# Expert choice and slot computation in fewer dependent rounds, four position products for nine, the first gather ahead of the block list

## The chip, the cores and the metric

One core of one Trainium2 chip runs the whole kernel. The metric is the device time of one execution in microseconds. Its engines are TensorE (PE, matrix products; PEld is its loading of weights), VectorE (DVE), ScalarE (ACT), GpSimd (POOL) and SyncE (SP, which here only starts transfers); they run their own instruction streams and meet at semaphores.

## What is computed

One layer of a decoder on 320 tokens (256 of a prompt, 8 x 8 of samples): conditioning, a pooling and an RWKV-7 mixer, and a mixture of experts, all in float32. The change touches the routing of the mixture of experts, which reads in the reference:

```python
scores = sigmoid(h @ w_router)                        # (320, 16)
sel = scores + b_router
gscore = sum(top_k(sel.reshape(T, 4, 4), 2)[0], -1)   # the two best of each group of four
gbest = argmax(gscore, -1)
_, idx = top_k(where(in_group, sel, -inf), 2)         # the two best experts of the best group
wts = take_along_axis(scores, idx, 1); wts = wts / sum(wts)
...
dest = pstart[e_sorted] + (arange(A) - start[e_sorted])    # a slot for each token and expert
block_e = searchsorted(pend, arange(n_blocks) * block)     # the expert of each block
xb = h[toks]
y = (silu(xb @ w_gate[e]) * (xb @ w_up[e])) @ w_down[e]    # 2048 -> 1024 -> 2048
```

Ties go to the lower index, in the group as among the experts. The kernel uses blocks of 64 slots. With these inputs every expert has one block, so that 16 blocks are computed, and w_gate, w_up and w_down of each of the 16 experts (8.4 MB a matrix) are read once.

## The kernel before

Everything around the change lies in `phase_mix`. It has two `nc.Block()`s, at L1451 and L1799. At the end of a block all engines drain and meet in a barrier; at the start of the second each loads a loop count from `bei` (L1800, L1801), which VectorE has written before.

**First block.** TensorE multiplies by w_out (L1520), transposes back, and the second norm follows. `mg` holds the normed tokens with features in partitions. L1572 computes the router's logits, L1577 transposes them, L1585 transposes `mg` into token rows, which ScalarE copies to `h2` (L1638, twelve copies, semaphore `hb_ev`). VectorE (L1696 to L1784) does the routing. Its helper `step(ins)` issues one instruction and waits until it is complete; `o.did(ins)` issues without waiting, and `o.settle()` waits for all that were issued. A **round** is what lies between two such waits. Tokens lie in partitions, in three tiles of 128, 128 and 64.

- *Choice* (L1703 to L1736): sums with the bias, group scores from maxima and minima of pairs (L1706 to L1716), their maximum (L1718), the first group that equals it, by a serial loop over four groups (L1722, L1723), the rank of each expert in its group by a loop over four experts (L1727, L1731), and `chosen`, ones and zeros of 3 x 16 per partition (L1735, and L1736, which clears the rows beyond the last token). Then `ch_ok`.
- *Position products* on TensorE (L1593, L1596): for each tile, how many earlier tokens chose the expert (`tri`, strictly triangular, and `ones`), and the totals. Meanwhile VectorE normalises the weights (L1738 to L1745).
- *Slots* (L1750 to L1780): blocks per expert, their running sum, the list of blocks `bei` for all engines, `dest`, and the two slots `d01` of every token; then the two weights `w01` of every token (L1782 to L1784).

**Second block.** VectorE's `picks(b)` (L1969 to L1977) turns `d01` into a selection matrix `pick` for the 64 slots of block b, in two rounds. TensorE's `gather(b)` (L1836) multiplies it with `h2`; ScalarE copies the result to `xs` (L1924, L1925), TensorE transposes it (L1845), VectorE copies it to `xt` (L1983), and the expert's products with gate and up follow (L1868), then those with down (L1901). Blocks are taken in pairs, and block b + 1 is gathered inside block b. After each pair `send_back` (L1855), VectorE (L1992) and GpSimd (L2075) add the results to the residual.

**Weights.** SyncE loads the 12 units of each block in order (L1421) into a ring of six; each load waits for `used` of its slot, which TensorE raises with the last product that reads the unit. The first six units are loaded during the first block of instructions, the seventh waits for the first expert products of the second.

## Time and profile before

| | us |
|---|---|
| three timed runs | 1896.6, 1899.9, 1900.6 |
| median | 1899.9 |
| profiled execution, its own time | 1895.1 |
| span of the profiled execution | 1893.6 |
| choice, products and slots, first VectorE work to last | 895.2 to 912.8 |
| expert loop, first expert product to the end | 927.6 to 1893.6 |

TensorE is busy for 93% of the span, VectorE for 28%, ScalarE for 18%, GpSimd for 17%. Times of rows count from the start of the span. In a row of the order of time stand the start, the duration of the group, the engine, the line, the operation with what it writes and reads, the shape (partitions x elements) and how many instructions the group has; in brackets, how long the engine had been idle and who ended that. "Clock" is the clock granted to TensorE: 1.00 is its upper level, 2.4 GHz, and 0.50 its lower, 1.2 GHz.

### The profile page before, as it was taken

To read this page: it belongs to the slowest core of one execution; us is meant where nothing else is said; L and a number is where in the kernel's file an instruction comes from. 1 tells how busy PE (TensorE), PEld (TensorE's weight loads), DVE (VectorE), ACT (ScalarE), POOL (GpSimd) and SP (SyncE) were. 2 spreads that over 40 slices of the span, in tenths; PEclk is the share of its full clock that TensorE was granted. 3 is DMA by queue.
4 is the path that set the end of the run, shared out by engine and by line. 5 is a ranking of instruction groups with operands and counts; after the bars stand their busy time and mean duration, and the time that the engine had idled before them with its cause. 6 is when DMAs were issued, how large, how long until landed. Compare 5 with 4: busy or idle time off the path is not lost.

```text
span 1893.6 us, 28830 instructions
## 1 busy us (share of the span) xinstructions
PE 1768.3 (93%) x11589; PEld 919.5 (49%) x11589; DVE 529.9 (28%) x1239; ACT 334.1 (18%) x715; POOL 323.0 (17%) x474
## 2 busy tenths in 40 slices
PE   4799999999999997998699999999999999999996
PEld 1357655556555664775243343533535335353352
DVE  2225146555655451113211201112011120111203
ACT  2001223332333231005011000110001100011012
POOL 0030012211222022000000402204022040220403
PEclk9899999999999998998899999999999999999998
DMA  9984277656576546741299999999999999999992
GB/s 315 409 313 121 66 223 232 215 166 211 184 247 187 172 141 173 228 155 45 95 428 428 427 427 428 428 429 429 421 427 430 427 428 421 430 427 428 430 425 106
DMA packets 172632, 573.94 MB, mean 303 GB/s; under 512 B 10643, under 2 KB 102125, under 8 KB 146883
## 3 DMA queue, kind: packets, MB, share of 16 engines
q1 hardware_dynamic: 168750, 563.76, 76.7%
q0 software_dynamic: 3200, 6.20, 1.1%
q10 hardware_dynamic: 631, 3.27, 0.6%
q8 instruction: 36, 0.59, 0.1%
q14 instruction: 15, 0.12, 0.0%
HBM read 567.78 MB, written 5.65 MB: 303 GB/s over the span
## 4 chain that ended last, share of the span: by engine, by line
PE 39%; DMA 6%; issue 4%; POOL 1%; ACT 1%; DVE 0%; POOLq 0%; SPq 0%; DVEq 0%
PE PS L1868 18%; PE PS L1901 10%; DMA ring<-in_w_up 6%; PE PS L1836 5%; PE PS L1855 4%; PE PS L1845 1%; POOL x L2075 1%; PE PS L1891 1%; ACT xs L1925 0%; ACT xs L1924 0%; POOLq L1787 0%; POOL pw L2061 0%; SPq L1421 0%; DVE x L2035 0%; DVE xt L1983 0%
## 5 line engine op out<-in xcount | busy, mean ns | idle before, releaser
L1868 PE MATMUL PS<-ring,xt 128*64 128x512 f32 x2048 | 492.3, 603 | 26.3 <-DMA ring<-in_w_up 24.7
L1868 PEld LDWEIGHTS PS<-ring,xt 128*64 128x64 f32 x2048 | 196.8, 138 | 288.1 <-issue 243.5
L2075 POOL TENSOR_TENSOR x<-x,tmp 128x512 f32<-128x512 f32 (+1 forms) x96 | 125.2, 1307 | 668.5 <-DVE tmp L1992 668.5
L1901 PE MATMUL PS<-ring,att 128*64 128x512 f32 x1024 | 227.5, 593 | 0.0
L753 PE MATMUL PS<-ring 128*64 128x320 f32 x1344 | 219.4, 440 | 2.7 <-DMA ring<-in_w_in 2.7
L1901 PEld LDWEIGHTS PS<-ring,att 128*64 128x64 f32 x1024 | 116.8, 137 | 95.6 <-issue 58.3
L1992 DVE TENSOR_TENSOR tmp<-PS,catT 128x512 f32<-128x512 f32 (+1 forms) x96 | 66.1, 689 | 299.7 <-PE PS L1855 296.2
L2003 DVE TENSOR_TENSOR sgt<-sgt,PS 64x1024 f32<-64x1024 f32 x16 | 19.4, 1212 | 424.6 <-ACT sgt L1931 424.6
L1520 PE MATMUL PS<-catT,ring 128*128 128x320 f32 x416 | 114.4, 437 | 7.1 <-DMA ring<-in_w_out 7.1
L1836 PE MATMUL PS<-h,pick 128*64 128x512 f32 x408 | 107.5, 600 | 10.4 <-DVE pick L1973 10.4
L753 PEld LDWEIGHTS PS<-ring 128*64 128x64 f32 x1344 | 82.3, 138 | 62.9 <-issue 25.4
L1931 ACT ACTIVATE sgt<-PS 64x1024 f32<-64x1024 f32 x16 | 16.3, 1017 | 538.8 <-PE PS L1868 538.8
L1855 PE MATMUL PS<-ysb,pwt 128*128 128x512 f32 (+1 forms) x192 | 105.5, 636 | 5.3 <-DVE tmp L1992 2.5
L2061 POOL TENSOR_SCALAR pw<-slotw,d,w 128x64 f32<-128x64 f32 x96 | 55.4, 592 | 277.0 <-issue 175.3
L1520 PEld LDWEIGHTS PS<-catT,ring 128*128 128x128 f32 x416 | 79.4, 192 | 40.8 <-issue 9.1
L1836 PEld LDWEIGHTS PS<-h,pick 128*64 128x64 f32 x408 | 40.6, 138 | 73.6 <-issue 63.1
L1942 ACT COPY ysb<-PS 64x1024 f32<-64x1024 f32 x32 | 32.2, 1007 | 212.8 <-PE PS L1901 212.6
L1855 PEld LDWEIGHTS PS<-ysb,pwt 128*128 128x128 f32 (+1 forms) x192 | 28.2, 173 | 77.0 <-issue 66.1
L419 PE MATMUL PS<-ring,silT 128*32 128x512 f32 x512 | 61.6, 598 | 0.0
L722 POOL TENSOR_TENSOR uvx<-uv,bmask 128x512 f32<-128x512 f32 x16 | 16.3, 1035 | 254.1 <-DVE uv L1318 254.1
L1110 ACT COPY zbd<-PS 64x320 f32<-64x320 f32 x80 | 33.5, 419 | 143.5 <-PE PS L902 143.0
L1269 DVE COPY_PREDICATED invt<-lvl_t,PS 64x320 f32<-64x320 int32 x80 | 41.4, 518 | 18.2 <-PE PS L902 14.9
(451 smaller groups left out, 1831.7 us busy)
## 6 DMA issues: line engine op xcount, KB each, us to landing
ring<-in_w_gate SPq DMA_DIRECT2D x64, 2048.0 KB, 12.5
ring<-in_w_up SPq DMA_DIRECT2D x64, 2048.0 KB, 16.2
ring<-in_w_down SPq DMA_DIRECT2D x64, 2048.0 KB, 15.7
ring<-in_w_ada SPq DMA_DIRECT2D x43, 2048.0 KB, 11.1
ring<-in_w_in SPq DMA_DIRECT2D x28, 1024.0 KB, 8.3
ring<-in_w_out SPq DMA_DIRECT2D x16, 1024.0 KB, 8.4
catT<-in_w_ada SPq DMA_DIRECT2D x5, 2048.0 KB, 11.5
ring<-in_w_in SPq DMA_DIRECT2D x1, 3072.0 KB, 20.4
```

What stands on the lines that cost most here:

```text
L419: m = nc.tensor.matmul(psum[32 * g:32 * g + 32, :], silT[:, kt, :], abuf[:, u, k, :], start=(kt < 4), stop=(kt >= KT - 4))
L753: m = nc.tensor.matmul(PS[r, j, 0:T], wbuf[:, j, k, r], hT[:, k, :], start=(k == 0), stop=(k == KT - 1), skip_group_check=True)
L1110: m = nc.scalar.copy(zbd[r, :, h, :], cut(W[3][r, 0:T]))
L1269: return nc.vector.copy_predicated(dst, nc_, src)
L1520: m = nc.tensor.matmul(PS[:, j, 0:T], wo[:, j, k, :], catT[:, k, :], start=(k == 0), stop=(k == KT - 1))
L1836: m = nc.tensor.matmul(PS[C * (c % 2):C * (c % 2) + C, 4 + c // 2, :], pick[:, i, :], h2[:, i, 512 * c:512 * c + 512], start=(i == 0), sto ...
L1855: nc.tensor.matmul(PS[0:n_, 2 + r % 2, :], pwt[:, t0:t0 + n_], ysb[:, c, :], start=True, stop=True).then_inc(t_sc, 1)
L1868: m = nc.tensor.matmul(PS[C * g:C * g + C, c, :], xt[:, 4 * q + k, :], unit(2 * q + g, FE)[:, k, 512 * c:512 * c + 512], start=(q == 0 and ...
L1901: m = nc.tensor.matmul(PS[C * (c % 2):C * (c % 2) + C, 4 + c // 2, :], att[:, 2 * q + k, :], unit(u, D)[:, k, 512 * c:512 * c + 512], star ...
L1992: nc.vector.tensor_tensor(tmp[0:n_, r % 2, :], PS[0:n_, 2 + r % 2, :], gtm[0:n_, i // 2, 512 * c:512 * c + 512], ALU.mult).then_inc(sc_ev, 1)
L2061: m = nc.gpsimd.tensor_scalar(pw[:, k, i, :], slotw[:, :], d01[:, k, i:i + 1], w01[:, k, i:i + 1], ALU.is_equal, ALU.mult)
L2075: nc.gpsimd.tensor_tensor(xx, xx, tmp[0:n_, r % 2, :], ALU.add).then_inc(x_ok, 1)
```

## The change

- *Choice*: all comparisons of the four experts of a group with each other are made at once, 12 x 4 x 4 = 192 elements per partition, once "greater" (`over`) and once "equal" (`same`, kept where the rival has the lower index, `lower`); their sum over the rivals is the rank. The first best group comes from a product with 4, 3, 2, 1 (`first`) and a maximum. The rows beyond the last token are cleared in `rank`, beside another operation. VectorE waits for GpSimd's set-up earlier. Rounds up to `ch_ok`: 11 for 26.
- *Products*: four with up to 48 columns, in place of nine with 16; the totals stand per tile and are summed by VectorE.
- *Slots*: blocks per expert by one comparison with five thresholds (`steps`) and a sum; near and far slots side by side; `picks(0)` at once behind `d01`, and the block list and the weights `w01` behind `picks(0)`. From the totals to `pick`, 12 rounds in place of 25.
- *Gather*: `gather(0)` stands at the end of TensorE's first block, with a wait for ScalarE's twelfth copy to `h2`; so the barrier and the loads of the loop count, which stood ahead of `picks(0)` and `gather(0)`, stand behind both.
- `gather` and `picks` are moved up so that both blocks can call them, unchanged but for the engine as an argument. `be` now lies in a part of `gated_tile`.

```diff
@@ -1423,6 +1423,29 @@
+    def gather(pe, b):
+        pe.wait_ge(pick_ok, b + 1)
...
+    def picks(ve, b):
+        earlier(ve, t_pk, b)
...
@@ -1435,11 +1458,16 @@
-    cmp_ = mt("cmp", [P, 12, EPG])
+    over, same = mt("over", [P, 12, EPG, EPG]), mt("same", [P, 12, EPG, EPG])
+    lower, first, steps = mt("lower", [P, EPG, EPG]), mt("first", [P, NG]), mt("steps", [P, T // SLOT])
+    count = mt("count", [P, NE])
+    flat = over[:, :, :, :].rearrange("p a e j -> p (a e j)")
+    full = flat[:, 0:NE * (T // SLOT)].rearrange("p (e k) -> p e k", e=NE)
+    near, far = (flat[:, n:n + 3 * NE].rearrange("p (i e) -> p i e", i=3) for n in (96, 144))
...
-    be = mt("be", [1, 32, NE])
+    be = gated_tile[0:1, 1:3, :].rearrange("p j t -> p (j t)")[:, 0:32 * NE].rearrange("p (b e) -> p b e", b=32)
@@ -1502,6 +1530,13 @@
+            own(nc.gpsimd.memset(lower[:, :, :], 0.0))
+            for e in range(1, EPG):
+                own(nc.gpsimd.memset(lower[:, e, 0:e], 1.0))
+            for g in range(NG):
+                own(nc.gpsimd.memset(first[:, g:g + 1], float(NG - g)))
+            for k in range(T // SLOT):
+                own(nc.gpsimd.memset(steps[:, k:k + 1], float(k * SLOT if k else -1)))
             pool.sem_inc(p_own, 1)
@@ -1588,13 +1623,16 @@
-            for i in range(3):
-                for i2 in range(i + 1):
-                    nc.tensor.matmul(PS[:, 7, i * NE:(i + 1) * NE], tri[:, :] if i2 == i else ones[:, :],
-                                     chosen[:, i2, :], start=(i2 == 0), stop=(i2 == i))
-            for i in range(3):
-                m = nc.tensor.matmul(PS[:, 7, 48:64], ones[:, :], chosen[:, i, :], start=(i == 0), stop=(i == 2))
-            m.then_inc(t_pos, 1)
+            picked = chosen[:, :, :].rearrange("p i e -> p (i e)")
+            nc.tensor.matmul(PS[:, 7, 0:48], tri[:, :], picked, start=True, stop=False, skip_group_check=True)
+            nc.tensor.matmul(PS[:, 7, 16:48], ones[:, :], picked[:, 0:32], start=False, stop=False, skip_group_check=True)
+            nc.tensor.matmul(PS[:, 7, 32:48], ones[:, :], picked[:, 0:16], start=False, stop=True, skip_group_check=True)
+            nc.tensor.matmul(PS[:, 7, 48:96], ones[:, :], picked, start=True, stop=True, skip_group_check=True
+                             ).then_inc(t_pos, 1)
+
+            pe.wait_ge(hb_ev, 12)
+            gather(pe, 0)
+
@@ -1702,41 +1740,41 @@
+            rival = s4.unsqueeze(2).broadcast_to([P, 12, EPG, EPG])
+            mine = s4.unsqueeze(3).broadcast_to([P, 12, EPG, EPG])
             for n, (a, b, op) in enumerate(((0, 1, ALU.max), (0, 1, ALU.min), (2, 3, ALU.max), (2, 3, ALU.min))):
                 o.did(tt(r4[:, n, :], s4[:, :, a], s4[:, :, b], op))
-
-            o.did(nc.vector.memset(rank[:, :, :], 0.0))
-            o.did(nc.vector.memset(small[:, 1, :], 1.0))
+            o.did(tt(same[:, :, :, :], rival, mine, ALU.is_equal))
+            o.did(tt(over[:, :, :, :], rival, mine, ALU.is_gt))
             o.settle()
+            ve.wait_ge(p_own, 2)
             o.did(tt(r4[:, 4, :], r4[:, 0, :], r4[:, 2, :], ALU.max))
             o.did(tt(r4[:, 5, :], r4[:, 0, :], r4[:, 2, :], ALU.min))
             o.did(tt(r4[:, 6, :], r4[:, 1, :], r4[:, 3, :], ALU.max))
+            o.did(tt(same[:, :, :, :], same[:, :, :, :],
+                     lower[:, :, :].unsqueeze(1).broadcast_to([P, 12, EPG, EPG]), ALU.mult))
             o.settle()
-            step(tt(r4[:, 5, :], r4[:, 5, :], r4[:, 6, :], ALU.max))
-            step(tt(r4[:, 4, :], r4[:, 4, :], r4[:, 5, :], ALU.add))
+            o.did(tt(r4[:, 5, :], r4[:, 5, :], r4[:, 6, :], ALU.max))
+            o.did(tt(over[:, :, :, :], over[:, :, :, :], same[:, :, :, :], ALU.add))
+            o.settle()
+            o.did(tt(r4[:, 4, :], r4[:, 4, :], r4[:, 5, :], ALU.add))
+            o.did(nc.vector.tensor_reduce(rank[:, :, :], over[:, :, :, :], AX.X, ALU.add))
+            o.settle()
             gsc = r4[:, 4, :].rearrange("p (i g) -> p i g", g=NG)
-            step(nc.vector.tensor_reduce(small[:, 0, :], gsc, AX.X, ALU.max))
+            o.did(nc.vector.tensor_reduce(small[:, 0, :], gsc, AX.X, ALU.max))
+            o.did(nc.vector.memset(rank[C:P, 8:12, :], float(EPG)))
+            o.settle()
             eq = r4[:, 5, :].rearrange("p (i g) -> p i g", g=NG)
             step(tt(eq, gsc, small[:, 0, :].unsqueeze(2).broadcast_to([P, 3, NG]), ALU.is_equal))
-            for g in range(NG):
-                step(tt(eq[:, :, g], eq[:, :, g], small[:, 1, :], ALU.mult))
-                step(tt(small[:, 1, :], small[:, 1, :], eq[:, :, g], ALU.subtract))
-            for j in range(EPG):
-                for lo, hi, op in ((0, j, ALU.is_gt), (j + 1, EPG, ALU.is_ge)):
-                    if lo < hi:
-                        o.did(tt(cmp_[:, :, lo:hi], s4[:, :, j:j + 1].broadcast_to([P, 12, hi - lo]), s4[:, :, lo:hi], op))
-                o.settle()
-                for lo, hi in ((0, j), (j + 1, EPG)):
-                    if lo < hi:
-                        o.did(tt(rank[:, :, lo:hi], rank[:, :, lo:hi], cmp_[:, :, lo:hi], ALU.add))
-                o.settle()
-            step(ts(rank[:, :, :], rank[:, :, :], 2.0, None, ALU.is_lt))
+            step(tt(eq, eq, first[:, :].unsqueeze(1).broadcast_to([P, 3, NG]), ALU.mult))
+            step(nc.vector.tensor_reduce(small[:, 1, :], eq, AX.X, ALU.max))
+            step(tt(eq, eq, small[:, 1, :].unsqueeze(2).broadcast_to([P, 3, NG]), ALU.is_equal))
             c4 = chosen[:, :, :].rearrange("p i (g e) -> p (i g) e", e=EPG)
-            step(tt(c4, rank[:, :, :], r4[:, 5, :].unsqueeze(2).broadcast_to([P, 12, EPG]), ALU.mult))
-            step(nc.vector.memset(chosen[C:P, 2, :], 0.0))
+            step(nc.vector.scalar_tensor_tensor(out=c4, in0=rank[:, :, :], scalar=2.0,
+                                                in1=r4[:, 5, :].unsqueeze(2).broadcast_to([P, 12, EPG]),
+                                                op0=ALU.is_lt, op1=ALU.mult))
             ve.sem_inc(ch_ok, 1)
...
@@ -1745,43 +1783,48 @@
             ve.wait_ge(t_pos, 1)
-            ve.wait_ge(p_own, 2)
-            for k in range(T // SLOT):
-                step(nc.vector.scalar_tensor_tensor(out=nb[:, 0, :], in0=PS[:, 7, 48:64], scalar=float(k * SLOT),
-                                                    in1=nb[:, 0, :], op0=ALU.is_gt, op1=ALU.add))
-            step(ts(nb[:, 0, :], nb[:, 0, :], 1.0, None, ALU.max))
+            step(nc.vector.tensor_reduce(count[:, :], PS[:, 7, 48:96].rearrange("p (i e) -> p e i", i=3), AX.X, ALU.add))
+            step(tt(full[:, :, :], count[:, :].unsqueeze(2).broadcast_to([P, NE, T // SLOT]),
+                    steps[:, :].unsqueeze(1).broadcast_to([P, NE, T // SLOT]), ALU.is_gt))
+            step(nc.vector.tensor_reduce(nb[:, 0, :], full[:, :, :], AX.X, ALU.add))
             step(nc.vector.tensor_tensor_scan(nb[:, 1, :], nb[:, 3, :], nb[:, 0, :], 0.0, ALU.mult, ALU.add))
-            o.did(tt(nb[:, 2, :], nb[:, 1, :], nb[:, 0, :], ALU.subtract))
+            step(tt(nb[:, 2, :], nb[:, 1, :], nb[:, 0, :], ALU.subtract))
+            step(ts(nb[:, 2, :], nb[:, 2, :], float(SLOT), None, ALU.mult))
+            step(tt(dest[:, :, :], PS[:, 7, 0:48].rearrange("p (i e) -> p i e", e=NE),
+                    nb[:, 2, :].unsqueeze(1).broadcast_to([P, 3, NE]), ALU.add))
+            big = 8192.0
+            o.did(nc.vector.scalar_tensor_tensor(out=near[:, :, :], in0=dest[:, :, :], scalar=-big, in1=chosen[:, :, :],
+                                                 op0=ALU.add, op1=ALU.mult))
+            o.did(nc.vector.scalar_tensor_tensor(out=far[:, :, :], in0=dest[:, :, :], scalar=1.0, in1=chosen[:, :, :],
+                                                 op0=ALU.add, op1=ALU.mult))
+            o.settle()
+            o.did(nc.vector.tensor_reduce(d01[:, 0, :], near[:, :, :], AX.X, ALU.min))
+            o.did(nc.vector.tensor_reduce(d01[:, 1, :], far[:, :, :], AX.X, ALU.max))
+            o.settle()
+            o.did(ts(d01[:, 0, :], d01[:, 0, :], big, None, ALU.add))
+            o.did(ts(d01[:, 1, :], d01[:, 1, :], -1.0, None, ALU.add))
+            o.settle()
+            picks(ve, 0)
 
             o.did(tt(be[:, :, :], nb[0:1, 1, :].unsqueeze(1).broadcast_to([1, 32, NE]),
                      bnum[:, :].unsqueeze(2).broadcast_to([1, 32, NE]), ALU.is_le))
             o.did(tt(odd[:, :], bnum[:, 0:32:2], nb[0:1, 1, NE - 1:NE].broadcast_to([1, 16]), ALU.is_lt))
+            for v, k in ((near, 0), (far, 1)):
+                o.did(tt(v[:, :, :], dest[:, :, :], d01[:, k, :].unsqueeze(2).broadcast_to([P, 3, NE]), ALU.is_equal))
             o.settle()
-            o.did(ts(nb[:, 2, :], nb[:, 2, :], float(SLOT), None, ALU.mult))
             o.did(nc.vector.tensor_reduce(bef[:, :], be[:, :, :], AX.X, ALU.add))
             o.did(nc.vector.tensor_reduce(npair[:, 1:2], odd[:, :], AX.X, ALU.add))
+            for v in (near, far):
+                o.did(tt(v[:, :, :], v[:, :, :], wts[:, :, :], ALU.mult))
             o.settle()
             o.did(ts(npair[:, 0:1], npair[:, 1:2], 2.0, None, ALU.mult))
             o.did(ts(bef[:, :], bef[:, :], float(NE - 1), None, ALU.min))
-            o.did(tt(dest[:, :, :], PS[:, 7, 0:48].rearrange("p (i e) -> p i e", e=NE),
-                     nb[:, 2, :].unsqueeze(1).broadcast_to([P, 3, NE]), ALU.add))
+            for v, k in ((near, 0), (far, 1)):
+                o.did(nc.vector.tensor_reduce(w01[:, k, :], v[:, :, :], AX.X, ALU.add))
             o.settle()
             o.did(nc.vector.tensor_copy(bei[:, 0:32], bef[:, :]))
             o.did(nc.vector.tensor_copy(bei[:, 32:34], npair[:, :]))
-
-            big = 8192.0
-            step(ts(sel[:, :, :], dest[:, :, :], -1.0, big, ALU.mult, ALU.add))
-            step(tt(sel[:, :, :], sel[:, :, :], chosen[:, :, :], ALU.mult))
-            step(nc.vector.tensor_reduce(d01[:, 0, :], sel[:, :, :], AX.X, ALU.max))
-            o.did(ts(d01[:, 0, :], d01[:, 0, :], -1.0, big, ALU.mult, ALU.add))
-            step(ts(sel[:, :, :], dest[:, :, :], 1.0, None, ALU.add))
-            step(tt(sel[:, :, :], sel[:, :, :], chosen[:, :, :], ALU.mult))
-            step(nc.vector.tensor_reduce(d01[:, 1, :], sel[:, :, :], AX.X, ALU.max))
-            step(ts(d01[:, 1, :], d01[:, 1, :], -1.0, None, ALU.add))
-            for k in range(2):
-                step(tt(sel[:, :, :], dest[:, :, :], d01[:, k, :].unsqueeze(2).broadcast_to([P, 3, NE]), ALU.is_equal))
-                step(tt(sel[:, :, :], sel[:, :, :], wts[:, :, :], ALU.mult))
-                step(nc.vector.tensor_reduce(w01[:, k, :], sel[:, :, :], AX.X, ALU.add))
+            o.settle()
     mixing.close()
@@ -1827,16 +1870,6 @@
-            def gather(b):
...
@@ -1875,7 +1908,7 @@
-                gather(b + 1)
+                gather(pe, b + 1)
@@ -1905,7 +1938,6 @@
-            gather(0)
             gather_turn(0)
@@ -1962,21 +1994,6 @@
-            def picks(b):
...
@@ -1994,7 +2011,7 @@
-                picks(b + 1)
+                picks(ve, b + 1)
@@ -2009,7 +2026,6 @@
-            picks(0)
             turned(0)
```

## Rows read from the trace of the kernel before

**Rows 1.** Stretches: us, PE, PEld, DVE, ACT, POOL, clock, DMA share, GB/s

```profile
937.00:942.00 5.00, 5.00 (x26) 1.72 (x24) 0.00 (x0) 0.00 (x0) 0.00 (x0) 1.00 0.98 413
...
1001.00:1800.00 799.00, 779.96 (x3390) 348.99 (x3388) 128.94 (x238) 83.67 (x110) 167.80 (x196) 0.99 1.01 427
```

**Rows 2.** Who waited for whom, 920 to 1894: us in total, times, longest

```profile
PE PS L1868 <- DMA ring<-in_w_up: 24.7, 14, 2.7
```

**Rows 3.** Order of time, start of the expert loop: start, us, what, [idle before]

```profile
927.56 28.04 PE L1868 MATMUL PS<-ring,xt 128*64 128x512 f32 x128 [1.46 <-DVE xt L1983]
...
934.67 0.33 SPq L1421 DMA_DIRECT2D ring<-in_w_gate  x1
```

**Rows 4.** Order of time, choice of experts and the first position product

```profile
893.87 5.40 PE L1585 MATMUL PS<-ident,mg 128*128 128x128 f32 x48
...
895.07 5.84 ACT L1638 COPY h<-PS 128x512 f32<-128x512 f32 x12
895.20 0.21 DVE L1703 TENSOR_TENSOR sel<-scores,browt 128x48 f32<-128x48 f32 x1 [0.72 <-ACT scores L1633]
895.44 0.45 DVE L1706 TENSOR_TENSOR r<-sel 128x12 f32<-128x12 f32 x4
...
897.19 0.17 DVE L1722 TENSOR_TENSOR r<-r,small 128x3 f32<-128x3 f32 x1
897.39 0.16 DVE L1723 TENSOR_TENSOR small<-small,r 128x3 f32<-128x3 f32 x1
...
901.43 0.07 DVE L1736 MEMSET chosen<- 64x16 f32 x1
901.65 0.21 DVE L1738 TENSOR_TENSOR wts<-scores,chosen 128x48 f32<-128x48 f32 x1
...
901.71 0.37 PE L1593 MATMUL PS<-chosen,tri 128*128 128x16 f32 x2 [2.44 <-DVEq L1737]
```

**Rows 5.** Order of time, slots on VectorE

```profile
905.97 1.01 DVE L1750 SCALAR_TENSOR_TENSOR nb<-PS,nb 128x16 f32<-128x16 f32 x5 [3.17 <-PE PS L1596]
...
907.54 0.67 DVE L1756 TENSOR_TENSOR be<-nb,bnum 1x512 f32<-1x512 f32 x1
...
912.36 0.21 DVE L1783 TENSOR_TENSOR sel<-sel,wts 128x48 f32<-128x48 f32 x1
912.60 0.20 DVE L1784 TENSOR_REDUCE w<-sel 128x3 f32<-128x48 f32 x1
```

**Rows 6.** Order of time, selection matrices, gathers and the copy on ScalarE

```profile
914.31 0.70 DVE L1969 TENSOR_SCALAR pick<-slotf,d 128x64 f32<-128x64 f32 x3 [1.51 <-issue]
914.32 3.46 POOL L2061 TENSOR_SCALAR pw<-slotw,d,w 128x64 f32<-128x64 f32 x6 [175.34 <-issue]
...
915.90 7.81 PE L1836 MATMUL PS<-h,pick 128*64 128x512 f32 x24 [10.41 <-DVE pick L1973]
...
923.75 0.58 ACT L1924 COPY xs<-PS 128x512 f32<-128x512 f32 x1 [22.83 <-PE PS L1836]
...
927.42 0.57 DVE L1969 TENSOR_SCALAR pick<-slotf,d 128x64 f32<-128x64 f32 x3
...
955.39 6.23 PE L1836 MATMUL PS<-h,pick 128*64 128x512 f32 x24
```

**Rows 7.** Busy time by microsecond; the number before the DMA share is the clock

```profile
888.00:889.00 1.00, 1.00 (x5) 0.47 (x3) 0.00 (x0) 0.75 (x3) 0.00 (x0) 0.50 0.00 0
...
901.00:902.00 1.00, 0.29 (x3) 0.32 (x3) 0.72 (x7) 0.00 (x0) 0.00 (x0) 0.98 0.00 0
...
918.00:919.00 1.00, 1.00 (x4) 0.29 (x2) 0.00 (x0) 0.00 (x0) 0.80 (x2) 0.50 0.00 0
919.00:920.00 1.00, 1.00 (x6) 0.34 (x4) 0.00 (x0) 0.00 (x0) 0.05 (x1) 0.99 0.00 0
```

**Rows 8.** The block boundary (L1451): the drain of TensorE, duration in ns and start

```profile
L1451 PEldq DRAIN  x1: 3648/3648/3648, 901.9 to 901.9; - x1
```

**Rows 9.** The load of the loop count (L1801) on ScalarE

```profile
L1801 ACTq TENSOR_LOAD <-bei x1: 488/488/488, 913.3 to 913.3; - x1
```

More of the change, by code:

```diff
@@ L1736, in _ @@
-            step(nc.vector.memset(chosen[C:P, 2, :], 0.0))
+            step(nc.vector.scalar_tensor_tensor(out=c4, in0=rank[:, :, :], scalar=2.0,
+                                                in1=r4[:, 5, :].unsqueeze(2).broadcast_to([P, 12, EPG]),
+                                                op0=ALU.is_lt, op1=ALU.mult))
             ve.sem_inc(ch_ok, 1)
             o.did(tt(wts[:, :, :], scores[:, :, :], chosen[:, :, :], ALU.mult))
-            o.did(nc.vector.memset(nb[:, 0, :], 0.0))
@@ L1829, in _ @@
             n = pairs(pe)
-            def gather(b):
-                pe.wait_ge(pick_ok, b + 1)
-                for c in range(4):
-                    for i in range(3):
-                        m = nc.tensor.matmul(PS[C * (c % 2):C * (c % 2) + C, 4 + c // 2, :], pick[:, i, :],
-                                             h2[:, i, 512 * c:512 * c + 512], start=(i == 0), stop=(i == 2),
-                                             skip_group_check=True)
-                m.then_inc(t_pk, 1)
             def gather_turn(b):
```

29 lines of the change are left out of this document (17 added, 12 removed).

## The prediction

> **What bounds the kernel now.** I read three views, in this order. First the stretches of the expert loop [rows 1]: the DMA engines are busy for the whole of it (share 1.01) at 427 GB/s, and TensorE is busy for 780 of 799 us beside them. Both run close to full, so I then asked who waits for whom [rows 2]: TensorE waits for a weight transfer 14 times, 24.7 us in all. The loop is paced by its weights, and TensorE follows just behind. Nothing in the loop is changed, so the question is when it starts. Third, the order of time at its start [rows 3]: six of a block's twelve weight units lie in the ring beforehand; the seventh is asked for at 934.67, when TensorE has used up the first. From then on the DMA never rests (share 0.98 from 937 to 942, 1.01 later) [rows 1]. Hence the rule on which my sum rests: every microsecond by which the transfer of 934.67 starts earlier comes off the end of the kernel, and a microsecond saved on an engine later in the loop is worth nothing.
>
> What precedes 934.67 is one serial chain from 895.20, where VectorE gets the scores. In it the DMA moves nothing, so no transfer hides any of it. It has four links: choice of experts [rows 4], position products and slots [rows 5], the block boundary with the selection matrices and the gather [rows 6], and the copies, transposes and the first 16 expert products (32 instructions).
>
> **Prices on VectorE.** Two neighbouring rows give the price of a dependent round: 0.20 us with 3 elements per partition (897.19 to 897.39) [rows 4], 0.24 with 48 (912.36 to 912.60) [rows 5]. The operation with 512 elements took 0.67 against 0.21 for 48 [rows 5], so an element costs (0.67 − 0.21) / 464 = 1.0 ns. A round of 192 elements is then 0.24 + 0.144 = 0.39 us; of 80 elements, 0.27. Within a round an operation that waits for nobody takes 0.10 (12 elements, four in 0.45 [rows 4]), about 0.14 (48) or 0.28 (192): its duration less the part that overlaps, some 0.07 us.
>
> **Choice of experts.** Before: 895.20 to the first position product at 901.71, 6.51 us [rows 4]. After, from 895.20: sum with bias 0.24; four pair operations 0.41 plus two comparisons of 192 elements 0.28 + 0.39; three small ones 0.25 plus a product 0.39; two rounds of 0.08 + 0.39; the group maximum with the small memset beside it 0.22; four rounds of 0.20; the final choice 0.24. Sum: 4.16. From there to TensorE I take the old way, which is 0.20 (the memset ends at 901.50, the product starts at 901.71) [rows 4]. So 4.36, and the product starts at 899.56; **2.15 us saved**. The 192-element operations read with broadcasts over two inner dimensions, which no row shows. Lower bound 0 extra; upper bound, twice the price per element for the five of them, 5 x 0.19 = 1.0 us. I take 0, since the 512-element row is a broadcast too. TensorE is free then: its transposes end at 893.87 + 5.40 = 899.27 [rows 4]. The added wait on GpSimd's set-up is free: GpSimd has sat idle for 175 us by 914.32 [rows 6], and 13 small memsets before that use none of the path.
>
> **Position products.** Before: 901.71 to VectorE's first slot operation at 905.97, 4.26 us [rows 4, 5]: 18 matmul instructions (two for each of nine float32 products), and the clock falls to its lower level at 902 [rows 7]. After: four products, 8 instructions. While it has just been working at the upper level, TensorE passes a 128-column transpose every 5.40 / 48 = 0.11 us [rows 4]; 8 x 0.11 plus 0.2 for the last gives 1.1. VectorE meanwhile normalises the weights, five rounds of 0.24, 0.24, 0.20, 0.20 and 0.24, together 1.12, and the two end side by side. I take 1.15, **3.1 saved**. At the lower level an instruction takes (4.26 − 0.5) / 18 = 0.21, with 0.5 for the last one's end; 8 x 0.21 + 0.5 is 2.2, and the saving 2.05. I take the first, since the clock stood at the upper level until 902 after a rest of 2.4 us [rows 4, 7], and here the rest is 0.3.
>
> **Slots.** Before: 905.97 to the end of the last reduction at 912.80; the boundary, until 914.31; two rounds of selection matrices, until the gather starts at 915.90: 9.93 us [rows 5, 6]. After: count 0.24, thresholds 0.27, their sum 0.27, scan 0.23, subtract 0.20, times 64 0.20, destinations 0.22, near and far 0.38, two reductions 0.38, two corrections 0.28 = 2.67. Then the matrices: 1.59 before, when GpSimd worked beside VectorE; with GpSimd idle the three first operations took 0.57 in place of 0.70 [rows 6], so I take 1.37, with 1.59 as the other end. Together 4.04; **5.9 saved**. The block list and the weights of the slots, taken off this path, cost about 2.9 us of VectorE behind the matrices. They lie under the gather of 7.8 us; without that cover they would cost their 2.9.
>
> The gather would thus start 2.15 + 3.1 + 5.9 = 11.15 us earlier, at 904.75. h2 is complete by 895.07 + 5.84 = 900.91 [rows 4], so its new wait is free.
>
> **What comes back.** The block boundary is not gone, it moves behind the gather. Before, ScalarE copied the gather's result 0.04 us after it ended (915.90 + 7.81 to 923.75) [rows 6]. Now TensorE reaches the barrier last, and what is queued behind it on ScalarE is the load of the loop count and then that copy. VectorE was the last then: 1.5 us from its end at 912.80 to its work at 914.31 [rows 5, 6]. ScalarE's load stands at 913.3 and takes 0.49 [rows 9], so its work can start some 0.3 us before that of VectorE, whose own end also took longer to be told than TensorE's: the drain of TensorE lasts just until its products are done (901.9 + 3.65 = 905.55) [rows 8]. Bounds 0.9 and 1.5 us. I take 1.15 more than before. GpSimd now builds its slot weights while VectorE copies the transposed tokens (1.29 us); by the ratio 0.70 / 0.57 that is up to 0.3, and I take 0.1, as that copy reads PSUM.
>
> **Sum:** 11.15 − 1.15 − 0.1 = **9.9 us**, with the gather as long as before. The gather ran its first three microseconds at the lower clock, until 919 [rows 7], and this adds 7.81 − 6.23 = 1.6 us against a later one [rows 6]. It now follows a rest of 4.1 us in place of 10, and can be anything from 6.2 to about 8.3. I keep 7.8.
>
> **The clock behind the gather.** From the gather's end to the first expert product, TensorE had only eight transposes in 3.8 us (923.71 to 927.56) [rows 3, 6], and what came next ran at the upper level's pace from the start (128 instructions in 28.04). The boundary stretches that to 5.0 us. In the rows the clock stood at the lower level during a microsecond full of transposes of h (888 to 889), yet it was still at the upper one at 901 to 902, behind 5.4 us of transposes of mg and 2.4 us of rest [rows 4, 7]. The Trainium skill (TensorE: Matmul & The Clock Gate, Part 4: PE-mode transpose) says that transposes don't count as work for the clock; by it the whole 5.0 us are rest and a fall is likely. The trace agrees for the rise and speaks against it for the fall.
>
> **Rivals.** (1) *The clock falls in those 5.0 us.* Then about 1.7 to 3.4 us of the first expert products, which release the seventh transfer, run at half speed: 0.8 to 1.7 lost, saving 8.6. For it: the longer rest. Against: the rows of 893 to 902. (2) *Cheap rounds are dearer than their small neighbours.* The five wide operations cost 1.0 more, the products run at the lower level (1.05 more), boundary and copies are at their dear ends (0.55), the clock falls too (1.3): saving 6.0. (3) *The gain is swallowed by a clock that stays low.* With less than full work between 899 and 917, the lower level could hold through gather and first products. The gather then takes 12.5 in place of 7.8, the first 16 products 14.0 in place of 7.0 (927.56 to 934.67, less 0.1) [rows 3], the small steps 0.3 more: 12.0, and the kernel is 2 us slower. If the level holds through the next 16 as well, ring slots come free 14.0 us apart while two units take 9.8 us (a unit is a quarter of an 8.4 MB matrix, and the rate 427 GB/s), the DMA starves for 4.2 more, and the kernel is 6 us slower. It decides from some 11 us of dense products at the lower level; the rows show 3 [rows 7]. (4) *The change doesn't shorten the start*, because the loop waits for something else. Against it stands the transfer of 934.67, issued when the 16th product ends (32 of the 128 instructions of 28.04 us are 7.0) and not before [rows 3]; 0 saved.
>
> **How the numbers follow.** Profiled execution: span 1893.6, time 1895.1, so 1.5 lie around it; after, span 1883.7 and 1885.2. The three timed runs have their median at 1899.9, 4.8 above the profiled one, and I forecast on that basis: 1899.9 − 9.9 = **1890.0**. Chances: forecast 0.55, (1) 0.27, (2) 0.10, (3) 0.05, half of it beyond 0.2%, (4) 0.03. Range: at the low end the profiled execution's basis with a warm gather too, 1884; at the high end case (2) on the median's basis, 1893.9, plus 1.1 for the scatter of a median, 1895. 0.2%, 3.8 us, is about what a measurement of this kernel can tell from no change; case (2) with scatter reaches it seldom. Faster 0.88, same 0.09, slower 0.03.
>
> **What would show it.** Right: first position product at 899.6, first slot operation at 900.7, gather at 904.8, ScalarE's copy 1.2 us behind its end, first transfer of the loop at 924.8, and the loop and the tail as long as before. Wrong: a wide comparison over 0.5 us, a clock at 0.50 in the first expert products, a gap in the DMA between 925 and 945, or a loop whose rate isn't 427 GB/s; a change of rate by 1% would be 9 us, as much as all of this.

## The result, and the profile after

Five timed runs of the changed kernel have their median at 1892.6 us, against 1899.0 for five of the kernel before; the ratio is 0.9965, with a 95% interval of 0.9952 to 0.9978. Two further sets on other occasions gave 0.9965 and 0.9961 (below). By the medians of the three sets the kernel is thus 6.4, 6.5 and 7.7 us faster, where 9.9 were forecast. (One of the five, at 3035 us with a granted clock of 0.56, is a disturbance and left out of the ratio.)

The order of time of the kernel after, from the scores on (start, duration, engine, line, operation), in the views that [rows 3 to 6] show of the kernel before:

```profile
897.23 0.21 DVE L1741 TENSOR_TENSOR sel<-scores,browt 128x48 f32<-128x48 f32 x1 [0.72 <-ACT scores L1671]
...
897.84 0.36 DVE L1747 TENSOR_TENSOR same<-sel 128x192 f32<-128x192 f32 x1
...
901.65 0.39 PE L1627 MATMUL PS<-chosen,tri 128*128 128x48 f32 x2 [0.35 <-DVEq L1776]
...
902.51 0.21 DVE L1783 TENSOR_TENSOR wts<-wts,small 128x48 f32<-128x48 f32 x1
902.82 0.21 DVE L1786 TENSOR_REDUCE count<-PS 128x16 f32<-128x48 f32 x1
...
905.47 0.58 DVE L1438 TENSOR_SCALAR pick<-slotf,d 128x64 f32<-128x64 f32 x3
...
906.90 8.72 PE L1430 MATMUL PS<-h,pick 128*64 128x512 f32 x24 [4.19 <-DVE pick L1442]
...
916.71 0.59 ACT L1956 COPY xs<-PS 128x512 f32<-128x512 f32 x1 [13.75 <-PEq L1479]
...
917.83 1.42 PE L1878 MATMUL PS<-ident,xs 128*128 128x128 f32 x8 [2.21 <-ACT xs L1957]
919.29 1.29 DVE L2000 COPY xt<-PS 128x512 f32<-128x512 f32 x2 [9.50 <-PE PS L1878]
...
920.63 14.65 PE L1901 MATMUL PS<-ring,xt 128*64 128x512 f32 x56 [1.38 <-DVE xt L2000]
...
930.16 0.33 SPq L1421 DMA_DIRECT2D ring<-in_w_gate  x1
```

Set beside the rows of before, this is where each link went. "Chain" is what lies between VectorE's first routing operation and the first transfer of the loop.

| link | before | after | saved | forecast |
|---|---|---|---|---|
| scores to position products | 6.51 | 4.42 | 2.1 | 2.15 |
| products to first slot operation | 4.26 | 1.17 | 3.1 | 3.1 |
| slots, block list, boundary, matrices, to the gather | 9.93 | 4.08 | 5.85 | 5.9 |
| gather | 7.81 | 8.72 | −0.9 | 0 |
| gather's end to ScalarE's copy | 0.04 | 1.09 | −1.05 | −1.15 |
| copy to first expert product | 3.81 | 3.92 | −0.1 | −0.1 |
| first 16 expert products, to the transfer | 7.11 | 9.53 | −2.4 | 0 |
| chain | 39.47 | 32.93 | 6.5 | 9.9 |

Every link on VectorE and the boundary came within 0.1 us. VectorE's work on the tokens' weights lies beside the products as forecast: it ends at 902.72, the slots start at 902.82. What is missing, 3.3 us, was lost in gather and expert products while TensorE was at its lower clock. These are the stretches of the kernel after, in the view of [rows 7], with the granted clock in the column before the DMA share:

```profile
902.80:906.90 4.10, 0.00 (x0) 0.03 (x1) 3.67 (x20) 0.15 (x1) 0.00 (x0) 0.77 0.01 2
906.90:911.90 5.00, 5.00 (x10) 1.65 (x12) 2.76 (x15) 0.00 (x0) 0.00 (x0) 0.50 0.00 0
911.90:915.60 3.70, 3.70 (x16) 1.16 (x12) 0.00 (x0) 0.00 (x0) 0.00 (x0) 1.00 0.00 0
915.60:918.70 3.10, 0.89 (x8) 0.87 (x8) 0.00 (x0) 1.07 (x2) 1.77 (x4) 1.00 0.00 0
918.70:920.60 1.90, 0.55 (x3) 0.17 (x2) 1.31 (x3) 0.00 (x0) 1.82 (x4) 0.50 0.00 0
920.60:925.50 4.90, 4.87 (x12) 1.48 (x14) 1.64 (x7) 0.00 (x0) 0.82 (x2) 0.50 0.00 0
```

The clock falls twice: in the pause ahead of the gather, so that the gather runs at the lower clock for 5.0 us (10 instructions in 5.0 us, then 16 in 3.7), and in the pause behind it, so that the first expert products do for 4.9.

The profiled spans differ by 2.6 us only (1893.6 and 1891.0), less than the chain. Two things outside the change account for it. The routing started 2.0 us later in this execution (897.23 against 895.20). And the last 16 gate and up products of the last block, behind TensorE's last wait for weights, met a lower clock and took 8.78 us in place of 7.09. The first line is of the kernel after, the second of the kernel before:

```profile
1826.58 8.78 PE L1901 MATMUL PS<-ring,xt 128*64 128x512 f32 x32 [2.70 <-DMA ring<-in_w_up]
```

```profile
1831.19 7.09 PE L1868 MATMUL PS<-ring,xt 128*64 128x512 f32 x32 [1.59 <-DMA ring<-in_w_up]
```

So −6.5 + 2.0 + 1.7 = −2.8, near the −2.6 measured. The 1.7 comes and goes whatever the kernel: those products take 8.78 us in seven of the fourteen traces of this document and 7.09 in the others, the repetition of the changed kernel (e0, span 1886.1) among them. One profiled execution can't give a difference of some microseconds between kernels; its links can.

### The profile page after: what moved, and what is told of

Same layout as the page of the kernel before. It is cut to its first block, busy times and chain, and to the rows that moved or that the text cites. A ratio compares the mean times of both kernels' runs of the same rounds, so it can differ in the third digit from the quotient of the medians.

```text
span 1891.0 us, 28803 instructions
## 1 busy us (share of the span) xinstructions
PE 1771.9 (94%) x11579; PEld 918.1 (49%) x11579; DVE 527.9 (28%) x1218; ACT 334.4 (18%) x715; POOL 324.6 (17%) x487
## 4 chain that ended last, share of the span: by engine, by line
PE 39%; DMA 6%; issue 4%; POOL 1%; ACT 1%; DVE 0%; POOLq 0%; SPq 0%; ACTq 0%
PE PS L1901 18%; PE PS L1934 10%; DMA ring<-in_w_up 6%; PE PS L1430 5%; PE PS L1888 4%; PE PS L1878 1%; POOL x L2091 1%; PE PS L1924 1%; ACT xs L1957 0%; ACT xs L1956 0%; POOLq L1830 0%; POOL pw L2077 0%; SPq L1421 0%; DVE x L2051 0%; DVE xt L2000 0%
```

## The experiments

Theory A: the end follows the first transfer of the loop, and the missing 3.3 us are the price of TensorE's pauses, of which the one behind the gather became longer (3.85 to 5.0 us) by the boundary. Theory B: the falls are chance, the change has no part in them. Every experiment has one trace and some timed runs. Ratios are to the kernel before, with runs of both on the same chip. "Pause" is from the gather's end to the first expert product, and "stretch" from the first transfer of the loop to the start of the last block's last 16 gate and up products (before: 896.5). Times are from one trace each, ratios from the timed runs:

| kernel | pause | gather | first 16 | chain | stretch | ratio |
|---|---|---|---|---|---|---|
| before | 3.85 | 7.81 | 7.11 | 39.5 | 896.5 | |
| changed | 5.0 | 8.72 | 9.53 | 32.9 | 896.4 | 0.9965 |
| e0 changed | 5.4 | 8.23 | 9.09 | 32.4 | 896.4 | 0.9965 |
| e11 changed | 5.0 | 8.69 | 9.51 | 32.9 | 895.2 | 0.9961 |
| e1 choice alone | 3.8 | 8.61 | 10.04 | 39.1 | 895.4 | 0.9990 |
| e2 without the move | 3.8 | 7.76 | 7.11 | 32.8 | 895.6 | 0.9968 |
| e3 move alone | 4.8 | 7.64 | 7.11 | 37.2 | 897.1 | 1.0000 |
| e5 late loads | 4.0 | 8.39 | 7.12 | 29.2 | 896.1 | 0.9948 |
| e10 late loads | 4.0 | 8.86 | 10.09 | 32.7 | 896.1 | 0.9961 |
| e4 filled, too much | 6.6, filled | 6.28 | 7.11 | 32.0 | 895.5 | 0.9953 |
| e9 pauses filled | 4.8, filled | 6.28 | 7.11 | 27.8 | 895.6 | 0.9933 |
| e8 filled, late loads | 4.0, filled | 6.28 | 7.11 | 27.0 | 896.3 | 0.9932 |
| e6 delay in front | 4.8, then ten extra products | 8.97 | 7.11 | 42.0 | 896.1 | 1.0004 |
| e7 delay in the loop | 5.3 | 8.38 | 9.22 | 32.6 | 898.0 | 0.9978 |

**The changed kernel again (e0, e11).** No edit.

> The changed kernel once more, unchanged. In its first profile the start of the loop came 6.5 us sooner on the chain (scores to first transfer of the loop, 32.9 us in place of 39.5), where 9.9 were forecast; the clock stood at its lower level in the second half of the pause behind the gather and in half of the 16 expert products before that transfer (9.5 us in place of 7.1), and longer in the gather (8.7 in place of 7.8). Theory A, the fall belongs to the longer pause behind the gather: it is here again, the first 16 products take 8.5 to 10 us, the chain 32 to 34. Theory B, it was chance of one execution: the products take 7.1, the chain 30. Ratio to before: A 0.9965, B 0.995.

> The changed kernel a third time, on the chip of the other three. Four traces with its pause behind the gather (twice the kernel itself, and the two with extra products in other places) all had the clock low in the first expert products: 9.1 to 9.5 us, or 11.5 for ten extra products in place of 8.7. Theory, the fall goes with the pause of 5 us: again 9 or more, chain 32.4 to 33. Rival, chance: 7.1, chain 30 to 30.5. Ratio 0.9965.

Measured: chains of 32.4 and 32.9, ratios 0.9965 (0.9953 to 0.9977) and 0.9961 (0.9947 to 0.9974). In all three traces the clock fell behind the gather, and the gather was 8.2 to 8.7 us long. The forecast of 9.9 fails each time by the same term.

**The choice alone (e1).** The kernel before with the new lines from `s4` to `ch_ok`, and `lower` and `first` set up (`be` lies in `gated_tile` here too).

> The kernel before with the new choice of experts alone. Scores to first position product 4.4 us in place of 6.5 (the changed kernel showed 4.42), the rest of the chain as before: chain 37.3 in place of 39.5, ratio 0.9989. Theory that the pauses decide: the clock is as in the kernel before, since no pause of TensorE behind the products is longer; gather 7.8, first 16 products 7.1. Rival, the shorter rest ahead of the position products keeps the clock up for them: 1.5 to 2 us more off the chain.

Measured: ratio 0.9990 (0.9981 to 0.9999). Scores to products 4.42, as expected. But the nine old products then took less as well, and this is the more useful reading:

```profile
902.31 0.36 PE L1599 MATMUL PS<-chosen,tri 128*128 128x16 f32 x2 [0.35 <-DVEq L1744]
...
903.64 0.82 PE L1602 MATMUL PS<-chosen,ones 128*128 128x16 f32 x6
904.57 1.01 DVE L1757 SCALAR_TENSOR_TENSOR nb<-PS,nb 128x16 f32<-128x16 f32 x5 [1.16 <-PE PS L1602]
```

904.57 − 902.31 = 2.26 us for the old products, in place of 4.26 before: TensorE came to them after a rest of 0.35 us in place of 2.44, and ran all of them at its upper clock. Of the 3.1 us that I put down to four products in place of nine, 2.0 belong to the quicker choice ahead of them and 1.1 to the products. The expected rival held in its size. Its reason, the shorter rest, is not what the clock shows: in the eleven traces without extra products ahead of the gather the clock first falls 6.7 to 8.3 us behind VectorE's first routing operation (6.7 before, 7.7 in e1, 6.8 in e3), whether the products start 4.4 or 6.5 us behind it. The quicker choice puts the products ahead of that fall: in e1 VectorE has them at 904.57, and the clock falls at 905.6. The clock also fell behind this gather, with a pause of 3.8 us, which had not changed: the first 16 products took 10.04, so that the chain was hardly shorter (39.1) although 4.1 us had gone from its first two links.

```profile
926.94 9.58 PE L1875 MATMUL PS<-ring,xt 128*64 128x512 f32 x30 [1.45 <-DVE xt L1990]
```

30 instructions in 9.58 us, where 40 took 8.80 in the kernel before.

**Without the move (e2)** and **the move alone (e3).** The edit shown is e2's, against the changed kernel; e3 makes the reverse of it in the kernel before.

```diff
-            pe.wait_ge(hb_ev, 12)
-            gather(pe, 0)
...
-            picks(ve, 0)
...
             pe.sem_inc(t_sc, NBK)
+            gather(pe, 0)
...
             ve.sem_inc(sc_ev, 2 + NBK)
+            picks(ve, 0)
```

> The changed kernel with selection matrices and first gather back in the second block, behind the block list, the slot weights and the boundary. Slot chain 2.7, block list and weights 2.9, boundary 1.5, matrices 1.6: the gather starts 8.7 us after the first slot operation, in place of 4.0 with the move and 9.9 before. The pause between gather and expert products is 3.8 again. Theory A (the fall belongs to the longer pause): gather 7.8, first 16 products 7.1, chain 33.0, as long as that of the changed kernel although the gather starts 4.7 us later. Theory B (chance): chain 33.0 too, but the changed kernel's repeat shows 30. Ratio 0.9965.

> The kernel before with the move alone: selection matrices right behind the slots of the tokens, the weights of the slots behind them, the gather at the end of the first block; choice, products and block list as before. By the rows: 1.45 us of weights off the path, 0.2 from matrices without GpSimd beside them, 1.5 of boundary removed ahead of the gather and 1.1 added behind it: 2.05 us off the chain, 37.4, ratio 0.9989. Theory A: the longer pause costs 2.4 us in the first products, the chain is 39.8 and nothing is gained, ratio 1.000. Theory B: 0.9989.

Measured: e2 0.9968 (0.9956 to 0.9980), with a gather that starts 8.5 us behind the first slot operation in place of 4.1; e3 1.0000 (0.9991 to 1.0009). With e0's 0.9965 this says that the move of gather and matrices has brought nothing that can be measured. It puts the gather 4.4 us earlier and gives back 1.05 at the boundary and, in the traces of e0 and e11, 0.5 to 0.9 in the gather, 0.1 to 0.5 in copies and transposes, and 2.0 to 2.4 in the first products. Theory A expected this, but one row speaks against its simple form: in e3 the pause was 4.8 us and the clock stayed up.

```profile
923.80:928.60 4.80, 1.24 (x10) 1.05 (x10) 1.36 (x3) 1.07 (x2) 3.45 (x7) 1.00 0.00 0
928.60:935.70 7.10, 7.10 (x34) 2.48 (x36) 1.63 (x7) 0.00 (x0) 0.93 (x2) 1.00 0.00 0
```

The trace of e3 and its timed runs don't say the same: its chain is 2.3 us shorter, which would be a ratio of 0.9988, and the interval begins at 0.9991. The mean granted clock of its eleven timed runs is 0.9695, against 0.9705 for the 22 of the kernel before beside them, and the traced execution has 0.971. So the traced one was probably lucky, and the clock fell behind the gather in others, of which there is no trace.

**Late loads of the loop count (e5, e10).**

```diff
+            gather_out(0)
             n = pairs(act)
...
+            gather_turn(0)
             n = pairs(pe)
...
+            turned(0)
             n = pairs(ve)
```

> The changed kernel, with the loads of the loop count on ScalarE, TensorE and VectorE put behind the copy of the first gather, its transposes and the copy to xt; the barrier stays. The gather's end to ScalarE's copy is 1.1 us in the changed kernel. Theory, the load is 0.7 of it (0.49 + 0.18 + 0.03) and the barrier the rest: 0.35 to 0.4 remain, chain 0.7 shorter and the pause as well, so that the clock falls less often. Rival: the barrier itself is the cost, the copy starts 1.1 after the gather as before. Ratio 0.996.

> The kernel with late loads once more. Its first trace had no fall of the clock behind the gather (chain 29.2). Theory, the pause there is 4.0 us, about as in the kernel before (3.8), and falls are as rare as there: chain 29 to 30, first 16 products 7.1. Rival, it was the luck of one execution: 31 to 32, first 16 products 9 or more. Ratio 0.995 by the first, 0.9955 by the second.

Measured: in e5 the copy starts at 915.79, and the gather ends at 907.11 + 8.39 = 915.50:

```profile
907.11 8.39 PE L1430 MATMUL PS<-h,pick 128*64 128x512 f32 x24 [4.20 <-DVE pick L1442]
...
915.79 0.58 ACT L1954 COPY xs<-PS 128x512 f32<-128x512 f32 x1 [12.65 <-PEq L1479]
```

0.29 us in place of 1.09: the barrier costs 0.3, the load of the count 0.8. The two traces of this kernel disagree on the clock, with the same pause of 4.0 us: 7.12 us of first products in one, 10.09 in the other. The ratios, 0.9948 (0.9934 to 0.9961) and 0.9961 (0.9947 to 0.9975), were taken on two chips and overlap. On e10's chip the changed kernel has 0.9961 as well (e11), so no gain of the late loads shows in the timed runs. The expectation of e10, that falls are rare with that pause, missed.

```profile
915.50:919.50 4.00, 1.23 (x8) 1.03 (x8) 1.32 (x3) 1.07 (x2) 2.70 (x5) 1.00 0.00 0
919.50:926.60 7.10, 7.08 (x34) 2.50 (x36) 1.80 (x7) 0.00 (x0) 1.68 (x4) 1.00 0.00 0
```

```profile
916.60:919.80 3.20, 1.23 (x8) 1.04 (x8) 0.54 (x1) 1.07 (x2) 1.92 (x4) 1.00 0.00 0
919.80:926.60 6.80, 5.99 (x14) 1.71 (x16) 2.58 (x9) 0.00 (x0) 2.46 (x5) 0.50 0.00 0
```

**Filled pauses (e4, e9, e8).** Products that nobody reads, into a free bank, in the changed kernel (e4, e9), and with late loads (e8, one product at the second place, behind the barrier, too).

```diff
             pe.wait_ge(hb_ev, 12)
+            for _ in range(4):          # e4: 7
+                nc.tensor.matmul(PS[:, 0, :], ident[:, :], h2[:, 0, 0:512], start=True, stop=True)
             gather(pe, 0)
...
+            for _ in range(2):          # e4: 4
+                nc.tensor.matmul(PS[:, 0, :], ident[:, :], h2[:, 0, 0:512], start=True, stop=True)
             n = pairs(pe)
...
             gather_turn(0)
+            nc.tensor.matmul(PS[:, 0, :], ident[:, :], h2[:, 0, 0:512], start=True, stop=True)     # e4: 2
```

> The changed kernel with products that nobody reads (identity times 512 columns of h2, into a free PSUM bank) in TensorE's pauses: seven ahead of the first gather, four at the start of the second block, two behind the transposes of the gathered rows. Two traces of the changed kernel had the clock at its lower level for the first 5 to 6 us of the gather (8.2 and 8.7 us long) and for the first 4 to 5 us of the expert products (9.1 and 9.5). Theory A, TensorE's pauses cost this: gather 6.2, first 16 products 7.1, chain from scores to first transfer of the loop 28.5 in place of 32.4 and 32.9, ratio to before 0.9945. Rival, the clock is low there whatever TensorE does: the extra products run at half speed too and delay gather and expert products, chain 33 to 36, ratio 0.997 or above.

> The changed kernel with the extra products alone, in their right size (four, two, one), loads of the loop count as in the changed kernel. Theory, the clock costs 3.5 to 4.5 us of the chain: gather 6.3 long and 4.1 behind the first slot operation, first 16 products 7.1; chain 28.1, ratio 0.9945. Rival, the clock costs less than the products that hold it up: chain 32 or more, ratio 0.9965.

> The changed kernel with the loads of the loop count late and with extra products of the right size. In the run before, an extra product (two instructions) took 0.87 us, not 0.43, so that seven of them held the gather up by 2.3 us; here four stand ahead of the gather, one at the start of the second block, one behind the transposes. Theory, boundary and clock add up: gather 4.1 us behind the first slot operation and 6.3 long, copy 0.3 behind it, first 16 products 7.1; chain 27.3 in place of 32.4 to 32.9, ratio to before 0.994. Rival, the extra products collide with the path even so: chain 29 or more, no better than the late loads alone (29.2).

Measured: e4 0.9953 (0.9940 to 0.9967), gather 6.28 and first products 7.11, but the extra products were too many: an instruction of theirs takes 0.44 us (14 in 6.28), and the gather came 6.4 us behind the first slot operation in place of 4.1, so that the chain was 32.0 where 28.5 had been expected. In their right size they hold nothing up. The answer of e8:

```profile
903.58 3.70 PE L1635 MATMUL PS<-h,ident 128*128 128x512 f32 x8 [0.30 <-ACT h L1678]
907.39 6.28 PE L1430 MATMUL PS<-h,pick 128*64 128x512 f32 x24
913.99 1.10 PE L1882 MATMUL PS<-h,ident 128*128 128x512 f32 x2 [0.32 <-PEq L1479]
915.09 1.23 PE L1878 MATMUL PS<-ident,xs 128*128 128x128 f32 x8
916.16 1.02 PE L1885 MATMUL PS<-h,ident 128*128 128x512 f32 x2
917.70 18.67 PE L1908 MATMUL PS<-ring,xt 128*64 128x512 f32 x86 [0.52 <-DVE xt L2004]
```

and its clock over the same time:

```profile
903.50:907.40 3.90, 3.71 (x9) 1.45 (x9) 3.48 (x20) 0.03 (x1) 0.00 (x0) 1.00 0.00 2
907.40:913.70 6.30, 6.27 (x24) 2.28 (x24) 2.84 (x15) 0.00 (x0) 0.00 (x0) 1.00 0.00 0
913.70:917.70 4.00, 3.18 (x12) 1.56 (x13) 1.34 (x3) 1.07 (x2) 2.72 (x5) 1.00 0.00 0
917.70:924.80 7.10, 7.10 (x34) 2.49 (x36) 1.78 (x7) 0.00 (x0) 1.65 (x4) 1.00 0.00 0
```

The ratios are 0.9933 (0.9919 to 0.9947) for e9 and 0.9932 (0.9918 to 0.9946) for e8, against 0.9961 for the changed kernel on the same chip: medians 1885.5 and 1884.7 against 1890.6 and, before, 1898.3. With extra work and nothing taken away, the kernel is 5.2 us faster than the changed one (e9), which is what the clock cost it (chain 32.9 less 27.8 = 5.1). The timed runs bear the traces out: the mean granted clock is 0.974 to 0.976 in all fifteen of e4, e9 and e8, and 0.970 to 0.973 in all fifteen that make up the ratios of the changed kernel. e8 is the fastest of all; the 0.8 us by which its chain is shorter than e9's can't be told in the ratios.

**A delay ahead of the first transfer (e6) and behind it (e7).** Ten extra products in the changed kernel: in e6 behind `gather_turn(0)` and a wait for `xt`, in e7, as shown, inside the first block of experts, behind its `gather_turn`.

```diff
+                if isinstance(j, int) and h == 0:
+                    for _ in range(10):
+                        nc.tensor.matmul(PS[:, 0, :], ident[:, :], h2[:, 0, 0:512], start=True, stop=True)
```

> The changed kernel with ten products that nobody reads, 4.3 us at the upper clock, behind the transposes of the first gather and ahead of the first expert product. Theory, the first transfer of the loop sets the end: it starts 4.3 us later (up to 2.4 less where the extra products take the slow stretch of the clock in place of expert products, and up to 2.4 more where they run slowly themselves), the stretch from that transfer to the last 16 products of the last block stays 896.4 as in both traces of the changed kernel, and the kernel is 2 to 6 us slower than the changed one: ratio to before 0.998 to 0.9995. Rival, TensorE's 25 us of waits for weights absorb it: ratio 0.9965.

> The changed kernel with the same ten products later, in the first block behind the transposes of the second gather, where the DMA already runs. Theory, the loop is paced by the DMA: TensorE is 4.3 us late there, makes it up at its next waits for weights, the stretch from first transfer to the last products stays 896.4, ratio 0.9965 as for the changed kernel. Rival, TensorE paces the loop: 4.3 us longer, stretch 900.7, ratio 0.9988.

The ten took twice what I had assumed, 8.8 us at the upper clock:

```profile
921.76 11.49 PE L1944 MATMUL PS<-h,ident 128*128 128x512 f32 x20 [1.38 <-DVE xt L2003]
...
940.29 0.33 SPq L1421 DMA_DIRECT2D ring<-in_w_gate  x1
```

```profile
958.62 8.75 PE L1921 MATMUL PS<-h,ident 128*128 128x512 f32 x20
```

e6: 11.49 us, as they took over the slow stretch, after which the first 16 products needed 7.11. The chain is 42.0, 9.1 more than 32.9; the stretch is 896.1, the same; ratio 1.0004 (0.9994 to 1.0013), 0.39% or 7 us above that of the changed kernel. A delay ahead of the first transfer is paid in full, within the intervals. e7: 8.75 us later in the loop, of which the stretch shows 898.0 − 896.4 = 1.6 (2.8 against the 895.2 of e11), and the ratio, 0.9978 (0.9969 to 0.9987), some 2.5 with intervals that overlap. Most is absorbed; the rest has a row of its own, in the DMA share, before the last number:

```profile
970.00:980.00 10.00, 10.00 (x49) 6.43 (x47) 0.00 (x0) 0.00 (x0) 2.71 (x6) 1.00 0.79 303
```

Here the DMA engines stood idle for 2.1 us (0.21 of 10), while in the changed kernel the same ten microseconds have a share of 1.00. I read this as the limit of the ring: the DMA paces the loop until TensorE is later than its six units cover.

## Why the prediction was right, and where it was not

The time lies in the range (1892.6 in 1884 to 1895), and the direction is the one forecast. That it lies in the range is luck in part: the saving of 6.4 us is nearer to the 6.0 of case (2), which set the upper end, than to 9.9, and of the terms of case (2) only the fall of the clock came, at nearly twice its 1.3 us. By its steps:

- **The end follows the first transfer of the loop.** Right. Over thirteen of the fourteen traces of the table the chain goes from 42.0 down to 27.0, and the stretch behind it stays within 895.2 to 897.1; the fourteenth is e7. e6 shows a delay paid in full. "Worth nothing later in the loop" is right for TensorE only while the ring covers it (e7).
- **Prices per round and per element.** Right: 4.42 for 4.36, and the comparison of 192 elements took 0.36 with its broadcasts over two inner dimensions. I had bounded the extra price of the broadcasts at 1.0 us in all and taken none of it, which held.
- **Products.** The sum of 3.1 is right and its owner is wrong: e1 shows 2.0 of it as the clock, since the quicker choice puts the products ahead of its fall, and 1.1 as fewer instructions.
- **Slots, matrices, cover of the block list.** Right, 4.08 for 4.04; the two rounds of matrices took 0.58 and 0.68 us of work without GpSimd beside them, and 1.43 to the gather in place of 1.37. The block list ends at 909.80, under a gather that ends at 915.62.
- **Boundary behind the gather.** Right, 1.09, where 1.15 more than the 0.04 of before was forecast. The small term for VectorE's copy beside GpSimd was not needed: that copy took 1.29 as before. The 0.1 by which the link grew came from transposes of which the last ran at the lower clock (1.42 in place of 1.23).
- **Gather as long as before.** Wrong by 0.4 to 0.9. I gave 6.2 to 8.3, kept 7.8, and two of the three traces of the changed kernel lie above even that (8.72 and 8.69). Before, the gather began when 14 us of lower clock were behind it and 3 ahead; now the clock falls 1.8 to 2.8 us before the gather, and 4 to 5 us of the lower stretch lie in it.
- **The clock stays up behind the gather.** This is the step that failed. I gave the fall, rival (1), a chance of 0.27; it is in all three traces of the changed kernel, a clock at 0.50 in the first expert products, as the list of signs of being wrong has it. Its price was too low as well, 2.0 to 2.4 us in place of 0.8 to 1.7: the products ran at the lower clock for 4.9 us in the kernel after, and no row had shown the 1.7 to 3.4 of the prediction. Together with the gather that is the 3.3 that are missing from 9.9. I took the upper clock of 901 to 902, behind transposes alone, as evidence against a fall [rows 7]. The Trainium skill (TensorE: Matmul & The Clock Gate, Part 4: PE-mode transpose), by which transposes are no work for the clock, was weighed and set aside. The falls in the pauses of e0, e11 and e10, which hold nothing but transposes, fit it; e3 and e5, with such pauses and no fall, don't decide it; and in the kernel before and in e3 the clock stayed up through 5.4 us of transposes of mg and the 2.4 us of rest behind them, which speaks against it.

**What stays open.** Filling the pauses kept the clock up in all three kernels that did it, and gave back 5 us where the filling had the right size; so the pauses are a cause of the low stretches. That the longer pause is what makes the fall behind the gather so frequent is not shown: with pauses of 4.8 to 5.4 us it came in the three traces of the changed kernel and in those of e7 (first 16 products 9.22) and e6 (in the extra products), and not in e3; with 3.8 to 4.0 it came in e1 and e10, not in the kernel before, e2 and e5. The direction fits, the number of traces is too small. Another thing divides the same eleven traces at least as well: how long the gather had run at the upper clock when it ended. It was 4.7 us in the kernel before, 4.8 in e2 and in e3, without a fall; 3.5 to 3.9 in the kernel after, e11, e1, e10 and e6, with a fall in each; and 4.1 to 4.2 in e5 without one and in e0 and e7 with one. By that the move would bring the second fall because the first one takes up more of the gather, not because the boundary lengthens the pause, and neither e1 nor e3 would be an exception. No run was made to hold the one fixed and change the other. The nearest are e5 and e7, 4.1 us in both, with pauses of 4.0 and 5.3 and a fall in e7 alone, which speaks for the pause.

The basis was treated rightly. The profiled execution of before lay 4.8 us below the median; in twelve of the thirteen other traces the routing starts 1.0 to 3.4 us later than its 895.20, and in one (e9) 4.6 later, with next to nothing changed ahead of it, so that it was an early one.

## What to carry to other kernels

Where a serial stretch ends in a stream of transfers that then paces all the rest, count every microsecond up to the first transfer as worth one and the rest as worth little, but count TensorE's clock within that stretch too: each link on another engine is a rest for it, and what follows the rest may be paid at half speed. Cutting the other engines' links gave back less here than it removed as long as the rests were not filled; a few products that nobody reads, sized by a traced duration to end before the path needs the engine, were worth more here than the choice and the products' own edit together (5 us against 2.1 and 1.1). When an operation is moved ahead of a block boundary, the boundary moves behind it: order the loads after it so that only the barrier remains on the path (0.8 us of the chain here, too little for the timed runs to show).

## What the runs showed of the hardware

- A shorter rest can cost more clock than a long one: gathers behind a rest of 4.2 us took 8.2 to 9.0 us in the seven of the table, and those of the kernel before, e2 and e3, behind 7.4 to 10.4 us, 7.6 to 7.8 (e1, 10.0 us and 8.61, is the exception). What differs is where the fall lies: 1.3 to 2.8 us ahead of the gather in the seven, and 7.2 us or more ahead of it in the others. In the kernel after the lower stretches lie at 905.0 to 911.9 and at 918.7 to 925.5, though the gather had begun at 906.9 and the expert products at 920.6.
- The barrier between two blocks took 0.3 us from TensorE's last product to ScalarE's first operation, and the load of a register from SBUF 0.8 more (e5 against the kernel after).
- A float32 matmul instruction with 128 columns of weights took 0.44 us (20 in 8.75), one of the expert products with 64 took 0.22 [rows 3], both with 512 columns streamed; the latter are written in turn to the lower and the upper 64 partitions. My extra products were twice too long in e4, e6 and e7 because I took the price of the second for the first.
